# Finishing the choice of experts per two heads, beside the key scores, in a two-layer streaming encoder

## The reference, cut to what matters

```python
q = (xr @ w_query).reshape(n, PEER_HEADS, 2, PEER_DHALF)      # 8 heads, two halves of 128
s = jnp.einsum('nhcd,ckd->nhck', q, sub_keys)                 # 128 key scores per half
s1, i1 = lax.top_k(s[:, :, 0], 16)
s2, i2 = lax.top_k(s[:, :, 1], 16)
cand_s = s1[..., :, None] + s2[..., None, :]                  # 256 candidates per head
cand_i = i1[..., :, None] * 128 + i2[..., None, :]
top_s, top_pos = lax.top_k(cand_s, 16)
eidx = take_along_axis(cand_i, top_pos)                       # 8 x 16 = 128 experts per token
gate = softmax(top_s)
h = gelu(einsum('nhkd,nd->nhk', expert_u[eidx], xr))
out = einsum('nhk,nhkd->nd', gate * h, expert_v[eidx])        # rows of 1024 float32
```

## Time and profile before

| | |
|---|---|
| median of 3 runs | 3126.95 us |
| lowest and highest run | 3125.84 and 3232.6 us |
| the profiled execution's own time | 3110.61 us |
| its span | 3108.8 us |
| instructions | 33005 |
| busy: TensorE, VectorE, ScalarE, GpSimd | 69%, 58%, 22%, 34% |
| DMA | 1039.60 MB, mean 334 GB/s |

### The profile page before, as it was taken

How to read it: one execution, slowest core, us unless ns; L and a number is a source line. 1 busy time by engine, 2 the same in 40 slices (tenths; PEclk the granted TensorE clock), 3 DMA queues, 4 the chain that set the end, 5 groups by cost and what they waited for, 6 DMA issues and landing times. The chain is left out here.

```text
span 3108.8 us, 33005 instructions
## 1 busy us (share of the span) xinstructions
PE 2152.5 (69%) x11433; PEld 1141.4 (37%) x11433; DVE 1792.3 (58%) x4150; ACT 672.7 (22%) x1953; POOL 1072.5 (34%) x1022
## 2 busy tenths in 40 slices
PE   6879897566776866757668585576666767545655
PEld 3337676424443532522225232234223434322222
DVE  2364537355885664683655755747835445865554
ACT  2122111121221221121521113411212321121111
POOL 1024222333354643333433333333333223344442
PEclk9989899678888987878779698888878888877787
DMA  3440330789979899989999999999999999889997
GB/s 132 156 177 33 145 113 24 290 342 390 383 290 412 344 391 419 407 328 419 397 397 419 391 369 415 357 413 419 372 400 369 419 403 414 328 316 420 420 420 325
DMA packets 154900, 1039.60 MB, mean 334 GB/s; under 512 B 18288, under 2 KB 19488, under 8 KB 36336
## 3 DMA queue, kind: packets, MB, share of 16 engines
q0 software_dynamic: 119152, 832.67, 67.0%
q1 hardware_dynamic: 35584, 204.82, 16.7%
HBM read 1007.53 MB, written 23.63 MB: 332 GB/s over the span
## 5 line engine op out<-in xcount | busy, mean ns | idle before, releaser
L1353 POOL DMA_INDIRECT fl_pairs<-in_peer_uv,fl_row_at x652 | 738.8, 1133 | 1275.8 <-PE fl_acc L1326 1142.4
L1326 PE MATMUL fl_acc<-fl_pairs,fl_diag 128*64 128x512 f32 x2608 | 840.7, 748 | 434.0 <-ACT fl_diag L1299 413.0
L1279 DVE CUSTOM_DVE_ANT_0 fl_pairs<-fl_pairs,fl_rows 128x1024 f32<-128x1024 f32 x652 | 795.5, 1240 | 448.1 <-DMA fl_pairs<-in_peer_uv,fl_row_at 447.1
L1326 PEld LDWEIGHTS fl_acc<-fl_pairs,fl_diag 128*64 128x64 f32 x2608 | 282.2, 162 | 838.6 <-issue 779.3
L1305 ACT ACTIVATE fl_acts<-fl_dots 128x2 f32<-128x2 f32 x384 | 78.1, 203 | 1282.5 <-DVE fl_dots L1279 1282.2
L1299 ACT ACTIVATE fl_diag<-constants_sb,fl_mix 128x64 f32<-128x64 f32 x768 | 224.5, 341 | 304.5 <-DVE fl_mix L1269 302.9
L1326 PE MATMUL fl_acc<-fl_more,fl_diag 128*64 128x512 f32 x464 | 155.7, 771 | 99.0 <-ACT fl_diag L1299 99.0
L1353 POOL DMA_INDIRECT fl_more<-in_peer_uv,fl_row_at x116 | 133.2, 1148 | 219.7 <-PE fl_acc L1326 198.7
L1279 DVE CUSTOM_DVE_ANT_0 fl_more<-fl_more,fl_rows 128x1024 f32<-128x1024 f32 x116 | 140.0, 1222 | 94.2 <-DMA fl_more<-in_peer_uv,fl_row_at 94.1
L1269 DVE TENSOR_TENSOR fl_mix<-fl_row_gate,fl_acts 128x2 f32<-128x2 f32 x384 | 73.1, 192 | 133.1 <-ACT fl_acts L1305 76.8
L1684 PE MATMUL aacc<-pc_piece,at_xT 128*128 128x512 f32 x288 | 138.3, 624 | 12.1 <-PEq L1611 12.1
(11 more groups left out here) (552 smaller groups left out, 2869.5 us busy)
## 6 DMA issues: line engine op xcount, KB each, us to landing
pc_piece<-in_kvq_by_pair SPq DMA_DIRECT2D x36, 1024.0 KB, 9.4
pc_piece<-in_query_by_head SPq DMA_DIRECT2D x32, 1024.0 KB, 9.4
pc_piece<-in_past_k SPq DMA_DIRECT2D x16, 1024.0 KB, 14.6
pc_piece<-in_past_v SPq DMA_DIRECT2D x16, 1024.0 KB, 12.6
ro_w_ring<-in_rwkv_w_rkv SPq DMA_DIRECT2D x24, 512.0 KB, 8.7
ops<-operands SPq DMA_DIRECT2D x12, 1024.0 KB, 10.6
pc_piece<-in_out_by_pair SPq DMA_DIRECT2D x12, 1024.0 KB, 9.3
fl_pairs<-in_peer_uv,fl_row_at POOLq DMA_INDIRECT x652, 15.3
```

Of the source, the lines that this page charges most:

```text
L1279: dve.tensor_tensor_reduce(pair, pair, self.rows[:, u % 2, j, :], 1.0, 0.0, ALU.mult, ALU.add, self.dots[:, u % 2, q, j:j + 1]).then_inc(* ...
L1326: mm = pe.matmul(self.acc[j * FOLD:(j + 1) * FOLD, half, :], self.diag[:, self.summed % self.DIAGS, j, :], self.pair(g)[:, D + half * HALF ...
L1353: pool.indirect_dma_start(self.pair(g), None, self.io["peer_uv"], bass.IndirectOffsetOnAxis(ap=self.row_at[:, u % TILES, j, q:q + 1], axis ...
```

## The change

What it does: (1) `Choice.rest` works on one group (two heads) and is called after `best_of` of each group, four times, with 41 yields a group and 164 in all, as one generator `Choice.steps` that goes on across stages; (2) in `key_scores` it is advanced 8 yields a tick from the arrival of the first scores, in the first tile 10 a tick, ending at tick 48 of 63; (3) expert numbers and gates have semaphores and ticks of their own: out, in, out, in on four successive ticks, the gathers waiting only for the expert numbers; (4) `mixing_weight` moves to before the first `prompt_attention`; (5) turns per stage and the `side`, `end` and `turn` numbers are set anew, with two gather numbers' worth of shift in where the 8-place ring ends (`NARROW`). The rest of the diff follows from these.

```diff
-    def rest(self, dve, u):
+    def rest(self, dve, u, group):
...
+        half = self.GROUP // 2
+        lists, heads = slice(group * self.GROUP, (group + 1) * self.GROUP), slice(group * half, (group + 1) * half)
+        slots = slice(heads.start * PTOP, heads.stop * PTOP)
...
-        yield from top16(dve, own, passed, [top[:, h, :] for h in range(PH)], ...)
+        yield from top16(dve, own, passed, [top[:, h, :] for h in range(half)], ...)
...
-        if u > 0:
-            dve.wait_ge(*flow.turn_out.at(32 * u))
-        yield from settle(dve, dve.tensor_tensor(flow.expert[:], found[:, 0, :], found[:, 1, :], ALU.add), own)
+        if u > 0 and group == 0:
+            dve.wait_ge(*flow.expert_out.at(16 * u))
+            dve.wait_ge(*flow.gate_out.at(16 * u))
+        dve.tensor_tensor(flow.expert[:, slots], found[:, 0, :], found[:, 1, :], ALU.add).then_inc(*flow.expert_done.by())
...
+    PARTS = 4
+    def steps(self, dve, u):
+        for group in range(self.PARTS):
+            while self.arrived <= group:
+                yield
+            yield from self.best_of(dve, self.scores, group)
+            yield from self.rest(dve, u, group)
...
-    NARROW = range(0, 196)
+    NARROW = range(0, 2 * 93 + 16)
...
-        for u, out_at, in_at in self.turns:
-            if out_at == n:
-                self.turn_rows_out(pool, u)
-            if in_at == n:
-                self.turn_rows_in(pool, u)
+        for u, first in self.turns:
+            if first == n:
+                self.experts_out(pool, u)
+            if first + 1 == n:
+                self.experts_in(pool, u)
+            if first + 2 == n:
+                self.gates_out(pool, u)
+            if first + 3 == n:
+                self.gates_in(pool, u)
...
-                pool.wait_ge(*self.turn_in.at(32 * GROUPS * (u + 1)))
+                pool.wait_ge(*self.expert_in.at(16 * GROUPS * (u + 1)))
...
+    def experts_out(self, pool, u):
+        pool.wait_ge(*self.expert_done.at(Choice.PARTS * (u + 1)))
+        pool.dma_start(self.core.turn_at[u], self.expert[:]).then_inc(*self.expert_out.by(16))
+    def gates_out(self, pool, u):
         pool.wait_ge(*self.soft_done.at(u + 1))
+        pool.dma_start(self.core.turn_gate[u], self.gate[:]).then_inc(*self.gate_out.by(16))
+    def experts_in(self, pool, u):
+        pool.wait_ge(*self.expert_out.at(16 * (u + 1)))
+        self.turned_in(pool, u, self.row_at, self.core.turn_at, self.expert_in)
         self.known = u + 1
+    def gates_in(self, pool, u):
+        pool.wait_ge(*self.gate_out.at(16 * (u + 1)))
+        self.turned_in(pool, u, self.row_gate, self.core.turn_gate, self.gate_in)
...
+    STEPS = 8
     def best(self, dve):
-        group = None
+        self.choice.begin(dve, self.u)
         for n in range(1, self.ticks + 1):
             if n % 4 == 2 and 2 < n <= self.HC + 2:
                 q = n // 4 - 1
                 dve.wait_ge(*self.s_done.at(q + 1))
-                group = self.choice.best_of(dve, self.choice.scores, q)
-            if group is not None:
-                advance(group, 5)
-            if n % 4 == 1 or n == self.ticks:
-                drain(group if group is not None else ())
+                self.choice.arrived = q + 1
+            if self.choice.arrived:
+                advance(self.flow.part, self.STEPS)
             self.flow.vector(dve, n)
...
     def gpsimd(self, pool, n):        # FirstTile; KNOWN = 48
-        if n == self.ticks:
-            self.flow.turn_rows_out(pool, 0)
-            self.flow.turn_rows_in(pool, 0)
+        if n == self.KNOWN + 2:
+            self.flow.experts_out(pool, 0)
+        if n == self.KNOWN + 4:
+            self.flow.experts_in(pool, 0)
+        if n == self.KNOWN + 6:
+            self.flow.gates_out(pool, 0)
+        if n == self.KNOWN + 8:
+            self.flow.gates_in(pool, 0)
...
-        mixing_weight(core, io, flow, neg_lam, 11)
-            second_tile(core, io, flow, x, rows, ops, [(13, {}), (21, {}), (23, {}), (36, dict(rows=((1, 1),)))])
+            second_tile(core, io, flow, x, rows, ops, [(12, {}), (20, {}), (22, {}), (34, dict(rows=((1, 1),)))])
...
-        (56, dict(choose=1, side=175, end=12, turn=((1, 15, 18),))), (64, {}), (82, {}), (90, {}), (92, {}), (99, {}), (101, {}), (110, {})])
+        (57, dict(side=324, end=4, turn=((1, 5),))), (66, {}), (85, {}), (93, {}), (95, {}), (103, {}), (105, {}), (114, {})])
-            (114, dict(rows=((2, 1),), choose=2, side=25)), (117, dict(side=35)), (130, dict(side=50, end=3, turn=((2, 5, 7),))), (136, {}),
-            (148, {}), (152, {}), (159, {}), (162, {}), (176, {})])
+            (118, dict(rows=((2, 1),), side=36)), (122, dict(side=36, end=3, turn=((2, 4),))), (136, {}), (142, {}),
+            (144, {}), (155, {}), (159, {}), (167, {}), (170, {}), (182, {})])
-            (180, dict(rows=((3, 1),), choose=3, side=20)), (182, dict(side=20)), (196, dict(side=50, end=9, turn=((3, 11, 13),))), (203, {}),
-            (215, {}), (219, {}), (226, {}), (229, {}), (242, {})])
+            (185, dict(rows=((3, 1),), side=36)), (187, dict(side=36, end=3, turn=((3, 4),))), (201, {}), (208, {}),
+            (219, {}), (223, {}), (230, {}), (233, {}), (245, {})])
-        (246, dict(rows=((4, 1),), choose=4, side=20)), (247, dict(side=20)), (259, dict(side=50, end=9, turn=((4, 11, 13),))), (263, {}),
-        (291, {}), (294, {}), (298, {}), (300, {}), (306, {})])
-    run_flow(core, flow, 14, 316, choose=5, side=80, end=11, rows=((5, 1),), turn=((5, 13, 14),))
+        (249, dict(rows=((4, 1),), side=36)), (250, dict(side=36, end=3, turn=((4, 4),))), (263, {}), (267, {}),
+        (294, {}), (297, {}), (302, {}), (304, {}), (311, {})])
+    run_flow(core, flow, 7, 316, side=80, end=3, rows=((5, 1),), turn=((5, 4),))
```

More of the change, by code:

```diff
@@ L1098, in __init__ @@
         self.top, self.top_at = sb("top", [P, PH, PTOP]), sb("top_at", [P, PH, PTOP], U32)
-        self.digit, self.digit_f = (x[:].rearrange("p (c m) k -> p c (m k)", c=2) for x in (self.best_at, self.best))
         self.found = sb("found", [P, 2, SLOTS])
@@ L1126, in rest @@
         yield from settle(dve, dve.tensor_tensor(cand.rearrange("p h (i j) -> p h i j", j=PTOP), two[:, :, 0, :].unsqueeze(3).broadcast_to(heads4),
                                                  two[:, :, 1, :].unsqueeze(2).broadcast_to(heads4), ALU.add), own)
-        yield from top16(dve, own, passed, [top[:, h, :] for h in range(PH)], [top_at[:, h, :] for h in range(PH)], [cand[:, h, :] for h in range(PH)])
-        flat = top_at[:].rearrange("p h k -> p (h k)")
+        yield from top16(dve, own, passed, [top[:, h, :] for h in range(half)], [top_at[:, h, :] for h in range(half)], [cand[:, h, :] for h in range(half)])
@@ L1130, in rest @@
+        flat = top_at.rearrange("p h k -> p (h k)")
         dve.tensor_scalar(digit[:, 0, :], flat, 4, None, ALU.logical_shift_right)
         yield from settle(dve, dve.tensor_scalar(digit[:, 1, :], flat, 15, None, ALU.bitwise_and), own)
-        yield from settle(dve, dve.tensor_copy(digit_f, digit[:]), own)
-        two_at = best_at_f[:].rearrange("p (h c) k -> p h c k", c=2)
+        yield from settle(dve, dve.tensor_copy(digit_f, digit), own)
+        two_at = best_at_f.rearrange("p (h c) k -> p h c k", c=2)
@@ L1136, in rest @@
         for c in range(2):
-            yield from settle(dve, dve.tensor_tensor(hot, core.const("iota").unsqueeze(1).broadcast_to([P, SLOTS, PTOP]),
-                                                     digit_f[:, c, :].unsqueeze(2).broadcast_to([P, SLOTS, PTOP]), ALU.is_equal), own)
+            yield from settle(dve, dve.tensor_tensor(hot, core.const("iota").unsqueeze(1).broadcast_to(wide3),
+                                                     digit_f[:, c, :].unsqueeze(2).broadcast_to(wide3), ALU.is_equal), own)
             yield from settle(dve, dve.tensor_tensor(hot4, hot4, two_at[:, :, c, :].unsqueeze(2).broadcast_to(heads4), ALU.mult), own)
@@ L1207, with plan @@
     TIGHT, LOOSE = (0, 1, 1, 1), (0,1,1,2)
-    def plan(self, ticks, last, side=0, end=None, choose=None, turn=(), rows=(), lead=0, lags=TIGHT):
+    def plan(self, ticks, last, side=0, end=None, turn=(), rows=(), lead=0, lags=TIGHT):
         self.lead = lead
@@ L1213, in plan @@
         self.side, self.end, self.turns, self.row_loads = side, end, turn, rows
-        if choose is not None:
-            self.u, self.part = choose, None
         self.start = len(self.dots_by)
@@ L1282, in vector @@
         if self.side:
-            if self.part is None:
-                self.part = self.choice.rest(dve, self.u)
             advance(self.part, self.side * n // self.ticks - self.side * (n - 1) // self.ticks)
@@ L2202, in key_scores @@
     with ExitStack() as ctx:
-        part = LateScores(core, io, flow, ctx, pieces, first, xT, choice, layer, f"late{layer}{t}")
+        part = LateScores(core, io, flow, ctx, pieces, first, xT, choice, layer, layer * TILES + t, f"late{layer}{t}")
```

(33 more changed lines are left out.)

46 lines of the change are left out of this document (23 added, 23 removed).

## The result

The changed kernel takes **3175.2 us** (median of 4 runs, 3172.2 to 3186.9) against 3126.4 for the kernel before (4 runs): ratio 1.0175, 95% interval [1.0157, 1.0193]. I had 3125 us. By the medians it is slower by 49 us: under 2%, but with an interval clear of 1, just above my range, and the first rival's 3175 is what came. A later set of runs gives 1.0165 [1.0125, 1.0205].

A forecast was written before the change was run, and what follows sets the result against it. The DMA stream of gathers was taken as the bound. Key stages +46 us (+96 − 50), given back −42, start −6, GpSimd's queue 0: −2 on the 3126.95 us median, so 3125 us; range 3083 to 3170.

The forecast's parts named there:

- the first rival: Key stages pay in full: landed rows are worth nothing, add 50 us, 3175 us; chance 0.22.
- The key stages' lengths: Five key stages, each with 31 us more VectorE work, last 94, 84, 91, 94, 81 us; excess over DMA 96 us.
- My own test: Key stages of 84 to 94 us, VectorE over 85% busy, DMA share near 0.85; under 80% means forecast wrong.
- What is given back: Stages behind the key stages lose `rest` and shorten: −14, −7, −4, −4, −13, together −42 us.
- the credit of −50: Key stages' ends: landed rows waiting for VectorE count as 10 us of DMA done ahead per stage, −50 us.
- the second's 3079: Second rival: key stages keep their lengths, the +46 goes, the −42 and −6 stay, 3079 us; chance 0.2.
- The start: End of tile 0's wide stage: transfers now happen before it ends, −6 us; bounds −14 and +10.
- GpSimd's queue: Sends in each mixer, queued with the gathers: roughly even, 0 us, bounds −4 to +18 each.
- a second full wait: Third rival, on GpSimd: five mixers at 9 us, 3170 us, or 3215 at the full 18; chance 0.13.
- The price of the split: `rest` on VectorE, cut in four: 36 + 8 = 44 us per mixer, from 6.2 us fixed cost plus 2.
- the 2 us for chained steps: Split `rest` on VectorE: instructions waiting for the one ahead cost 1.6 to 6 us more; 2 taken.
- VectorE's idle time swallows it: Rival in the key stages: VectorE's idle time absorbs the added work, stages keep their lengths, 3079 us; chance 0.2.

## Why the prediction was wrong

Laid end to end, the runs make a ladder: the kernel before 1; sends apart +0.85%; split +0.3; new first tile +0.2; choice into the key stages +0.8; new turns −0.4; together +1.75. Its middle rungs are no more than likely: only the first, and the one of the key stages, stand clear of their intervals. It is also one order out of many: the rung of the sends was measured where GpSimd's waits grow to 90 us, and the rung of the key stages takes them down to 35 again, so the two can't be read as prices that add up.

- **The key stages' lengths held, nearly.** They last 97, 86, 94, 94 and 83 us for 94, 84, 91, 94 and 81, 10 us more in all. That the excess reads +98 against +96 is luck: my 29 us for the last stage counts the 8 us in which its DMA is idle, and these are in the 3110.61 to which I added it. Counted as in the table, my lengths make +88. From the first scores on, VectorE's work plus the `rest` that fits in is the right way to size such a stage. My own test, VectorE over 85% busy, was not met, and two of the five stages are even under the 80% that I had called a sign of a wrong forecast: it is 78 to 82% of the whole stage, because the head before the first scores counts in it. Taken from the first scores on it is 90 to 92%, as in these two, which answer to the last two of the earlier trace rows:

```profile
2157.00:2234.50 77.50, 71.67 (x256) 0.78 0.97 397
2708.00:2776.60 68.60, 62.48 (x236) 0.83 0.58 218
```

- **What is given back held.** −42 predicted, −40 measured. Its parts are not all as I had them: u = 1 gave 17 for 14, u = 2 16 for 7, u = 3 and 4 nothing for 8, u = 5 10 for 13. In the second profile the sum is −33.5.
- **The step that failed is the credit of −50: "rows have landed that wait for VectorE ... 10 us of DMA done ahead per stage".** The rows did land. From the GB/s column, u = 2: 345 × 85.7 us is 29.6 MB against 403 × 61.0 = 24.6 in the same turns, 12 us at the full rate of 414; all five, with 2.07 MB a turn, make 34 us. But they bought no time. The stages behind gave 40 us for the 42 that I had without any credit, and all other stages 3 more; in the second profile it is 33 and 3. Moving turns out of the key stages, which should have cashed the credit, cost 0.9%, 27 us, more. So in place of 50 us the runs show about nothing, and a key stage pays its excess in full. Why no stage behind could use the rows is open in part. Behind the key stage of u = 2 came short stages with VectorE busy for 39 of 45 us, which could not go faster. Behind the others GpSimd paused for its writes, but it waited less than in the kernel before (35 us in all for 62), so longer waits can't be what ate the credit. This was the first rival's mechanism, which I gave 0.22; the digits of the earlier trace rows showed a full stream, and I read that as slack to be stored, not as a rate that must never be missed. My range, 3083 to 3170, left this rival's 3175 out, and the second's 3079 too, though I gave the two 0.42 together: 0.88 for the range did not fit them.
- **The start: −6 predicted, +10.6 in the profile, some 6 of it the change's.** I took the transfers' tail as what ends the stage. It did go (GpSimd had issued the experts' reads 25 us earlier), but the compressed choice made the stage's own work 11 us longer, and GpSimd waited for its end: the +10 of my bounds, not the −6. Of the 10.6, 4.5 are there before the choice begins, as shown above. By the run with the old first tile it is 0.2%, 6 us, with intervals that meet.
- **GpSimd's queue: 0 predicted**, "a second full wait" as rival. There was none: its waits went from 62 to 35 us. Both sends at once instead gain 0.36%, 11 us, not told apart from nothing. The 0.85% of the run that only parts the sends in the kernel before is clear of its interval, but there the waits are 90 us, and 13 of its 26 us stand in the key stages.
- **That 3175 came is luck in part.** The first rival's mechanism is the one that the runs show, but its sum counts the 8 us twice, has −6 for the start where 10.6 stand, and carries the 16 us by which the median of the kernel before lay above its profiled execution; the changed kernel's lies at it (3175.2 and 3174.9).
- **The price of the split** was 8 us per mixer, measured 5.9. The Trainium skill ("VectorE: DVE Perf Modes", on the fixed latency) says that small instructions each pay it, and the 166 ns above agree, against 147 from MAX8. By the same page's DRAIN rule, that a semaphore in such a row costs nothing extra, the split would have been 6 us, and the 5.9 agree: the 2 us for chained steps were not there.
- **The rival "VectorE's idle time swallows it" fell**: no key stage kept its length where the load passed the DMA's time.

## What to carry to other kernels

Where a stream must never starve, the load of the other engine has to stay below the stream's own time in every stage, not on average: where work that is moved takes a stage past the stream's time, the excess is paid in full, and what lands ahead meanwhile was no gain in any of these runs. Before moving work, list idle time per stage and put work into the stages that have the most of it; here thinning `rest` out into the projection stage gained 0.6% with the choice's numbers in four stages changed. A transfer's early issue is worth nothing if what it feeds waits for something else, as at the start.

## What the runs showed of the hardware

- A small write that GpSimd issues behind a row of gathers lands late. In the run with the sends apart GpSimd waits 22.4 us for it at u = 3, with gathers on their way, and 7.0 for the next, with two gathers issued in between; at the start of the changed kernel, with no gather queued, the read behind it was issued 2.6 us after it.
- On VectorE, a 512-element comparison takes 712 ns where a quarter of the 2048-element one is 588.
- 41 us of extra VectorE work, 34 of them beside a stream whose DMA share is 0.96, cost 24 us: more than half of it was paid, though VectorE is busy for only 58% of the span.
- Two executions of kernels that are the same up to there differed by 5 us at 400 us (396.4 and 401.4).
